# Recurrence of a hybrid block: the first corner behind KB's products, the moments in front of its copy, and second halves of X and XT loaded from ScalarE

## The reference

```python
def step(S, inp):
    r_t, w_t, k_t, v_t, kk_t, a_t = inp
    sa = jnp.einsum('bhvk,bhk->bhv', S, -kk_t)
    S = (S * w_t[:, :, None, :]
         + sa[..., None] * (kk_t * a_t)[:, :, None, :]
         + v_t[..., None] * k_t[:, :, None, :])
    return S, jnp.einsum('bhvk,bhk->bhv', S, r_t)
_, o = lax.scan(step, S0, xs)
mean = jnp.mean(o, axis=-1, keepdims=True)
var = jnp.mean(jnp.square(o - mean), axis=-1, keepdims=True)
o = ((o - mean) * lax.rsqrt(var + GN_EPS)).reshape(B, T, W)
```

## Time and profile before

| what | us |
|---|---|
| median of 3 runs | 1310.01 |
| lowest and highest | 1305.36, 1314.89 |
| profiled execution, its own time | 1319.53 |
| span of the profiled execution | 1317.7 |
| the recurrence's tiles in the profile | 358.1 to 568.0 |

### The profile page before, as it was taken

The page is one execution under the profiler, slowest core; times in us unless marked ns, Lnnn a source line. Parts: engine busy times, 40 slices in busy tenths (PEclk is TensorE's granted clock), DMA queues, the critical chain, the costliest instruction groups (busy, mean ns, idle before and its releaser), DMA issues.

```text
span 1317.7 us, 20551 instructions
## 1 busy us (share of the span) xinstructions
PE 1269.1 (96%) x8207; PEld 1040.8 (79%) x8207; DVE 829.4 (63%) x1247; ACT 480.1 (36%) x863; POOL 271.8 (21%) x210
## 2 busy tenths in 40 slices
PE   7999999989899999999999999999999999999996
PEld 6888888655688888778878888888888887888885
DVE  6856522289766877364485665666777676546765
ACT  6100033398422323233463333333333334333334
POOL 0465600034311112110003332233133200000001
PEclk9999999999987989699999999999999999999998
DMA  5576532300222232152213223214544577766643
GB/s 217 186 250 219 209 116 93 109 1 18 48 57 48 52 72 58 31 204 106 80 49 128 70 74 96 96 55 154 176 154 150 192 241 270 257 206 215 208 144 136
DMA packets 117627, 172.80 MB, mean 131 GB/s; under 512 B 55328, under 2 KB 59424, under 8 KB 117280
## 3 DMA queue, kind: packets, MB, share of 16 engines
q1 hardware_dynamic: 117536, 171.54, 39.4%
HBM read 119.57 MB, written 51.39 MB: 130 GB/s over the span
## 4 chain that ended last, share of the span: by engine, by line
PE 80%; DVE 9%; DMA 5%; ACT 3%; issue 2%; POOL 0%; SPq 0%; DVEq 0%; ACTq 0%; POOLq 0%
PE bank L2366 28%; PE bank L363 21%; PE bank L2470 14%; PE bank L468 2%; PE bank L1491 2%; PE bank L1416 2%; DMA hid_scratch<-rt 1%; PE bank L377 1%; PE bank L1262 1%; DMA inv_scratch<-LM 1%; DMA X<-inv_scratch 1%; PE bank L986 1%; DVE scores L1172 1%; PE bank L1497 1%; DMA v_scratch<-vo 1%
## 5 line engine op out<-in xcount | busy, mean ns | idle before, releaser
L2366 PE MATMUL bank<-thi,ahi 128*128 128x512 f32 x320 | 124.5, 389 | 0.0
L2366 PE MATMUL bank<-tlo,ahi 128*128 128x512 f32 x320 | 124.5, 389 | 0.0
L2366 PE MATMUL bank<-thi,alo 128*128 128x512 f32 x320 | 124.5, 389 | 0.0
L2470 PE MATMUL bank<-ch,dwh 128*128 128x512 f32 x308 | 120.4, 391 | 1.3 <-DVE dwl L2044 1.2
L2470 PE MATMUL bank<-ch,dwl 128*128 128x512 f32 x308 | 119.9, 389 | 0.0
L2470 PE MATMUL bank<-cl,dwh 128*128 128x512 f32 x308 | 119.9, 389 | 0.0
L342 DVE TENSOR_TENSOR ring_wlo<-ring_raw,ring_whi 128x1024 fp32r<-128x1024 f32 x30 | 40.1, 1336 | 124.4 <-ACT ring_whi L336 124.4
L363 PE MATMUL bank<-hhi,ring_whi 128*128 128x512 f32 x288 | 114.8, 399 | 0.0
L363 PE MATMUL bank<-hhi,ring_wlo 128*128 128x512 f32 x288 | 112.4, 390 | 0.0
L363 PE MATMUL bank<-hlo,ring_whi 128*128 128x512 f32 x288 | 112.3, 390 | 0.0
L2366 PE MATMUL bank<-x1hi,ahi 128*128 128x512 f32 x240 | 93.4, 389 | 0.0
(11 more groups left out here) (341 smaller groups left out, 2826.7 us busy)
## 6 DMA issues: line engine op xcount, KB each, us to landing
hraw<-hid_scratch SPq DMA_DIRECT2D x12, 1024.0 KB, 6.5
hid_scratch<-hid SPq DMA_DIRECT2D x22, 512.0 KB, 6.2
hid_scratch<-rt SPq DMA_DIRECT2D x11, 1024.0 KB, 4.9
dwr<-down_sums SPq DMA_DIRECT2D x16, 704.0 KB, 4.3
ring_raw<-in_w_in SPq DMA_DIRECT2D x20, 512.0 KB, 4.1
raw_a<-in_w_gate_up SPq DMA_DIRECT2D x20, 512.0 KB, 4.1
raw_b<-in_w_gate_up SPq DMA_DIRECT2D x20, 512.0 KB, 4.8
dwr<-in_w_down SPq DMA_DIRECT2D x12, 704.0 KB, 4.5
```

What stands on the lines that cost most here:

```text
L2366: mm = pe.matmul(b[:, :], w[:, k, :], m[:, k, :], start=opens and k == 0 and i == 0, stop=not (j, n) in parts and k == 3 and i == 2, skip_ ...
L2470: mm = pe.matmul(b[:, :], w[m % 2][:, k, :], a[:, k, :], start=opens and k == 0 and i == 0, stop=name not in PART2 and k == KF - 1 and i = ...
```

## The change

On TensorE, `corners(1)` moves behind `products_of(br, 1)` and behind the claim of bank 5, in all tiles, and the first half of the outputs' products moves from behind `cumulative` to right behind `corners(1)`. Tile 7 has two fillers where it had three. On VectorE, `moments(t-1)` goes in front of `first_corners(t)`, and `variance(t-1)` in front of `first_updates(t)`. From tile 1 on, ScalarE issues the second halves of X and XT, behind the scaling of the state and a wait for the inverse's landing in DRAM; SyncE keeps the first halves.

```diff
+        def half_image(eng, m, o, q, done):
+            eng.dma_start(m[q * HD:(q + 1) * HD, :, :],
+                          bass.AP(d_i.tensor, o + q * (2 * P + 1) * HD, [[2 * P, HD], [8 * IMG2, H], [1, HD]])
+                          ).then_inc(done, 16)
...
                 for m, o, done in ((X, P, s_xl), (XT, 0, s_xt)):
                     if t and m is XT:
                         C.result(sp, "U", t - 1)
-                    for q in range(2):
-                        sp.dma_start(m[q * HD:(q + 1) * HD, :, :],
-                                     bass.AP(d_i.tensor, o + q * (2 * P + 1) * HD, [[2 * P, HD], [8 * IMG2, H], [1, HD]])
-                                     ).then_inc(done, 16)
+                    half_image(sp, m, o, 0, done)
+                    if not t:
+                        half_image(sp, m, o, 1, done)
...
                 if not more:
                     C.emptied(pe, "S", t - 1)
-                    busy(bank[3], 3)
-                if t:
-                    corners(1, t)
+                    busy(bank[3], 2)
                 pe.wait_ge(s_vtk, 16 * t + 16)
                 for g in range(4):
                     C.emptied(pe, f"k{g}", t)
                 products_of(br, 1, *range(H)).then_inc(s_r, 1)
                 bo = C.claim(pe, "O", t)
+                corners(1, t)
+                products_of(bo, 0, *range(4))
                 if t == 0:
-                    corners(1, t)
-                    products_of(bo, 0, *range(4))
                     busy(C.claim(pe, "S", t), 1)
                 pe.wait_ge(s_xt, 32 * t + 32)
                 updates(1, t)
                 if t + 2 < NT:
                     cumulative(pe, t + 2)
-                if t:
-                    products_of(bo, 0, *range(4))
                 corners(2, t)
...
                     ins.then_inc(s_S, 1)
+                    act.wait_ge(s_img2, 16 * (t + 1) + 16)
+                    half_image(act, X, P, 1, s_xl)
+                    half_image(act, XT, 0, 1, s_xt)
...
             for t in range(NT):
+                if t:
+                    moments(t - 1)
                 first_corners(t)
                 if t:
-                    moments(t - 1)
+                    variance(t - 1)
                 first_updates(t)
-                if t:
-                    variance(t - 1)
```

## The result

The changed kernel takes 1339.32 us (median of 4 runs, 1337.71 to 1339.94); the kernel before took 1311.13 us (4 runs, 1305.36 to 1314.89). The ratio is 1.0232, with a 95% interval from 1.0183 to 1.0281: slower by about 2%. That it is slower is clear of the noise; whether by more than 2% is not.

What follows compares the result with a forecast made beforehand. TensorE, busy for 96% of the span, bounds the kernel through its waits, clock and work. 1319.5 us less 23.6 (old dips) and 2.7 (waits, filler) gives 1293.2; plus 36.9 for new dips, 1330 us; range 1297 to 1345.

Steps and rivals of the forecast that it cites:

- The wait: At the claim of O's bank, tiles 1 to 6: TensorE waits 0.6 us each for `moments`, +3.6 us in all.
- X: Ahead of the first corner: TensorE's waits for X's landing go, -4.9 us; X comes about 0.1 us early.
- The second corner: Right behind `cumulative`: its wait for L1662 is covered and costs nothing; without cover some 0.4 us.
- the step that costed the moved products at nothing: Ts1's copy behind four products instead of eight, and the second corner behind `cumulative`: both hidden, no cost.
- The loads: ScalarE issuing the second halves of X and XT: gain bounded by 0 and 0.63 us of X's arrival, taken as 0.
- A tile at the full clock: Tiles of the changed kernel with granted clock 1.00 would take 23.4 to 23.6 us.
- The clock: Tiles 1 to 6: five dips of TensorE's clock, three long and two short, 36.9 us on top of 1293.2 us.
- a thin head: Behind the wait in each tile: corner, products and narrow updates, 3.5 us with only 1.0 us of full-height work.
- B: Rival: dips as often as before, only -2.7 us counts; 1307 beside the median run, 1317 beside the profiled; chance 0.24.
- C: Rival: the shorter wait no longer brings the clock down, none or one dip left; 1293 to 1303 us; chance 0.18.

Runs made afterwards that it cites:

- the one with the thicker head: Changed kernel with the wait at the claim kept and one full-height filler between first corner and the four products, tiles 1 to 6: 1309.81 us, ratio 0.9961.
- the first experiment: Changed kernel with one line moved, the first corner ahead of the claim of O's bank: 1302.36 us, ratio 0.9942 to the kernel before.
- the fastest one: Changed kernel with the corner ahead of the claim, plus one full-height filler behind the first corner in tiles 1 to 6: 1296.72 us, ratio 0.9913.

## Why the prediction was right

**The wait.** The prediction put a wait of 0.6 us at the claim in each of tiles 1 to 6, caused by VectorE's masks and `moments`. It is there six times, 0.73 us each. The size was off by 0.13 us: the products start 0.1 us sooner behind `of_state` than the narrow corner did (475.66 - 474.67 = 0.99 us, against the 1.10 us taken from the earlier trace rows), and so end sooner. The corner itself starts 3.62 us after `of_state` began, where the prediction's own numbers give 443.21 - 439.60 = 3.61 us: VectorE's side of the sum was right.

**X.** No wait for X is left, with ScalarE's loads or without them, as forecast.

**The second corner.** "Covered in the same way" holds where `cumulative` stands in front of it; tiles 6 and 7 have none, and there TensorE waits 0.56 us for L1665. This is a miss of the step that costed the moved products at nothing: 1.1 us.

**The loads.** Taken at 0 us; the run without them is the changed kernel within its scatter. ScalarE issues in 0.58 to 0.88 us where 0.65 was assumed, inside an idle stretch that is still 6.27 us long.

**A tile at the full clock.** Forecast at 23.4 to 23.6 us. The changed kernel has no such tile, but the one with the thicker head has: 24.40 us with a filler of 0.97 us in it, so 23.43 us.

**The clock.** The direction came from this term alone, and it held: by the forecast, the change without dips would have been worth 2.7 us. The size came out too small. The rate of three tiles in four, taken over from the kernel before, gave five dips, three of them long, worth 36.9 us. The profile has six, four of them long. Against 23.6 us for a tile of this kernel at the full clock (an estimate: the first experiment's 22.9 us plus the wait of 0.73), tiles 1 to 5 lose 4.6 + 10.1 + 10.1 + 10.5 + 10.8 = 46 us, some 1.5 us of which are waits on issue; tile 6 adds about 4. So the term came to near 49 us, 12 us more than forecast. The profiled execution without it would take 1339.6 - 48.5 = 1291.1 us, 2 us less than the forecast 1293.2, and 12 less 2 gives the 9.5 us between 1330 and 1339.6. The rate was mis-sized for the reason that the prediction itself gave: in the kernel before a tile behind a dip has no wait for X and is safe, and here every head is alike. That should have raised the rate above the old one, not kept it. As to the count of dips in the kernel before: the earlier trace rows show the three of the recurrence; the fourth that the prediction counts, from 196.3 to 199.7 us, is too short for those slices.

**The cause.** The two conditions, a wait and a thin head, were argued from which tiles dipped, and on that evidence the call was partly luck. The four tiles that waited for X were not alike: tiles 1 and 4 had waits of 1.00 and 1.08 us on TensorE's own issue as well, and tile 3, with 1.28 us for X and none on issue, kept its clock. The prediction did not name these waits as a rival. In the changed kernel they come behind the falls or not at all, and the runs bear out both conditions there: removing the wait (by order or by a filler) ends the long dips in tiles 1 to 6, and thickening the head with the wait left in ends them in tiles 1 to 5, though not in tile 6. What the runs do not settle is why single tiles of the improved kernels still dip. Waits on TensorE's own issue stand next to most of these dips, no run was aimed at them, and no written order or semaphore explains them, although by the section on the kernel before nothing else sets the time of an instruction. Nor does the list of instructions alone decide. Ahead of the recurrence the kernel before and the fastest one have the same instructions and the same wait:

```profile
353.57 2.00 PE L1262 MATMUL bank<-arv,ab 64*128 64x256 f32 x16 [1.79 <-DVE arv L1292]
...
352.25 3.30 PE L1262 MATMUL bank<-arv,ab 64*128 64x256 f32 x16 [1.79 <-DVE arv L1292]
```

In the first, of the kernel before, the clock held; in the second it fell at 352.7 us, for 3.5 us, and it did so too in the kernel with the fillers in tiles 6 and 7. No 32x32 matmul runs there. So the prediction's sentence "Idleness alone is therefore not what tells them apart", read from one profile, does not hold for short dips. In all twelve profiles, the long dips, of 20 us and more, begin in the recurrence.

**The rivals.** Dips as often as before (B), and few dips (C), did not occur. The rule of the Trainium skill's page "TensorE: Matmul & The Clock Gate", section "Loop structure matters more than you think", that long DMA waits cool the engine, is not enough for this case: no wait of TensorE for a DMA is left in the changed kernel's head, the waits that are there last 0.73 us, and the clock fell in each tile.

## What to carry to other kernels

A move that takes one wait away may bring the instruction behind another one: here the corner went behind a bank's claim that it does not need, and one line, the corner ahead of the claim, turned +2% into -0.6%. Where TensorE runs many narrow matmuls, look at the granted clock by stage before counting waits: a tile lost some 10 us to the clock and less than 1 us to the wait beside it. If such a stretch can't be reordered, a full-height filler beside the narrow work can pay for itself: six of them, in the wait, took the changed kernel from 1339.3 to 1302.8 us. The fastest kernel here has six as well, and takes 1296.7 us where the kernel before took 1313.8, but most of that is the corner's place. Look also at the same stretch in more than one profile: a stretch that keeps its clock in one profile can lose it in another.

## What the runs showed of the hardware that was not expected

The clock fell while TensorE was busy for 2.67 of 3.40 us, and stayed down for most of a tile in which it was busy for 33.0 of 33.7 us; ahead of the recurrence it had stayed up at 4.84 of 8.00 us. The busy share in the profile is therefore no safe guide to the clock in this kernel. With a wait of 0.73 us left in place, 0.97 us of full-height work behind it kept four tiles in a row at 1.00, and did not keep the fifth and the sixth. The stretch ahead of the recurrence, which held in the kernel before, fell for 3.5 us in two of the other kernels, with the same instructions and the same wait of 1.79 us in front.
